# Eight weight slots each for two projections of a fused transformer kernel, loaded behind the projection before them

## What is computed

```python
def hybrid_mixer(h, w_in, ..., w_gdn_proj, sc_conv_w, w_sc_out, w_o):
    p = h @ w_in                                   # q, k, v, z, three short-conv inputs, two gates
    ...
    o = gated_delta_rule_chunked(q, k, v, g, beta) # recurrence, head by head, chunks of 64 tokens
    o = rms_norm(o, gdn_norm_w) * silu(z)
    y_a = o.reshape(b, s, V_W) @ w_gdn_proj        # second projection of the change
    y_b = (gb * causal_depthwise_conv(gc * xin, sc_conv_w)) @ w_sc_out   # first projection
    gate_a = sigmoid(p[..., GA_OFF:GB_OFF]); gate_b = sigmoid(p[..., GB_OFF:IN_COLS])
    return (gate_a * y_a + gate_b * y_b) @ w_o     # third projection

# around it: x = x + g1 * mixer(modulate(rms_norm(x), sh1, sc1)), then an FFN in the same form,
# a final norm, and two further blocks with mixers and FFNs of their own.
# mod = silu(c) @ w_ada + b_ada gives the shifts, scales and gates; w_ada_f those of the first final norm.
```

## Time and profile before

| | us |
|---|---|
| median of three runs | 1551.38 |
| lowest and highest run | 1547.10, 1552.73 |
| device time of the profiled execution | 1547.16 |
| its span | 1545.6 |
| PE busy (share of the span) | 1433.0 (93%) |
| VectorE (DVE) busy | 747.8 (48%) |
| ScalarE (ACT) busy | 644.4 (42%) |
| last instruction of the last head on PE ends | 472.94 |
| second projection on PE starts | 475.50 |
| third projection on PE starts | 527.69 |
| first FFN on PE starts | 563.38 |

### The profile page before, as it was taken

How to read it: one execution, slowest core, us unless ns; L and a number is a source line. 1 busy time by engine, 2 the same in 40 slices (tenths; PEclk the granted TensorE clock), 3 DMA queues, 4 the chain that set the end, 5 groups by cost and what they waited for, 6 DMA issues and landing times.

```text
span 1545.6 us, 27829 instructions
## 1 busy us (share of the span) xinstructions
PE 1433.0 (93%) x10169; PEld 1261.8 (82%) x10169; DVE 747.8 (48%) x1452; ACT 644.4 (42%) x1171; POOL 14.8 (1%) x81
## 2 busy tenths in 40 slices
PE   5999999999998889999979998899998899899997
PEld 2977888887885678899947777799997678799997
DVE  0666656666532144455456543655553122555553
ACT  3454544445322044445364432555542222555542
POOL 3000000000000000000000000000000000000000
PEclk9899999999998989999979999899999889899999
DMA  8666457564553759965639983466564125266562
GB/s 292 178 206 203 150 151 232 187 196 136 166 148 125 214 151 290 273 183 160 173 109 291 282 271 96 137 185 181 162 180 157 29 86 135 70 185 180 167 187 83
DMA packets 400010, 269.89 MB, mean 175 GB/s; under 512 B 9914, under 2 KB 357424, under 8 KB 399936
## 3 DMA queue, kind: packets, MB, share of 16 engines
q1 hardware_dynamic: 399936, 268.83, 58.6%
HBM read 267.75 MB, written 1.05 MB: 174 GB/s over the span
## 4 chain that ended last, share of the span: by engine, by line
PE 76%; DMA 8%; DVE 7%; ACT 4%; issue 2%; SPq 2%; DVEq 0%; ACTq 0%
PE bank L715 16%; PE bank L716 15%; PE bank L717 15%; PE bank L680 5%; DMA w_raw<-in_w_in 4%; PE bank L758 4%; PE bank L651 3%; PE bank L666 2%; PE bank L1080 1%; DMA big<-in_w_ada 1%; DMA ring<-in_w_gdn_proj 1%; PE bank L888 1%; DVE w_low L1658 1%; PE bank L889 1%; PE bank L1112 1%
## 5 line engine op out<-in xcount | busy, mean ns | idle before, releaser
L715 PE MATMUL bank<-h_parts,w_high 128*128 128x256 f32 x1824 | 550.5, 302 | 17.0 <-DVE h_parts L1674 15.4
L716 PE MATMUL bank<-h_parts,w_high 128*128 128x256 f32 x1824 | 523.1, 287 | 0.0
L717 PE MATMUL bank<-h_parts,w_low 128*128 128x256 f32 x1824 | 522.4, 286 | 0.0
L1658 DVE TENSOR_TENSOR w_low<-w_raw,w_high 128x1024 fp32r<-128x1024 f32 (+2 forms) x324 | 359.5, 1122 | 184.2 <-ACT w_high L1223 184.0
L715 PEld LDWEIGHTS bank<-h_parts,w_high 128*128 128x128 f32 x1824 | 355.7, 195 | 43.8 <-issue 25.3
L716 PEld LDWEIGHTS bank<-h_parts,w_high 128*128 128x128 f32 x1824 | 357.5, 196 | 3.9 <-issue 3.6
L717 PEld LDWEIGHTS bank<-h_parts,w_low 128*128 128x128 f32 x1824 | 356.7, 196 | 0.0
L1223 ACT ACTIVATE w_high<-w_raw 128x1024 fp32r<-128x1024 f32 (+2 forms) x324 | 312.6, 973 | 81.4 <-DMA w_raw<-in_w_in 38.0
L1215 ACT ACTIVATE evac<-bank 128x256 f32<-128x256 f32 x140 | 53.9, 385 | 232.9 <-PE bank L717 183.3
L715 PE MATMUL bank<-act_parts,w_high 128*128 128x256 f32 x528 | 149.3, 283 | 0.0
L717 PE MATMUL bank<-act_parts,w_low 128*128 128x256 f32 x528 | 148.6, 281 | 0.0
(11 more groups left out here) (338 smaller groups left out, 1495.6 us busy)
## 6 DMA issues: line engine op xcount, KB each, us to landing
w_raw<-in_ffn_w_in SPq DMA_DIRECT2D x88, 512.0 KB, 3.8
w_raw<-in_w_in SPq DMA_DIRECT2D x72, 512.0 KB, 4.0
ada_w<-in_ada_w SPq DMA_DIRECT2D x34, 1024.0 KB, 5.4
w_raw<-in_w_ffn_in SPq DMA_DIRECT2D x44, 512.0 KB, 6.4
ada_w<-in_w_ada SPq DMA_DIRECT2D x16, 1024.0 KB, 11.5
w_raw<-in_gla_w_in SPq DMA_DIRECT2D x24, 512.0 KB, 6.4
w_raw<-in_ffn_w_out SPq DMA_DIRECT2D x32, 384.0 KB, 3.8
w_raw<-in_ffn_w_out SPq DMA_DIRECT2D x32, 320.0 KB, 3.0
```

Source lines behind the costliest of these rows:

```text
L715: pe.matmul(acc[:, 0:T], hi[:, n, :], x_parts[:, k, 0, :], start=k == 0, stop=False)
L716: pe.matmul(acc[:, 0:T], hi[:, n, :], x_parts[:, k, 1, :], start=False, stop=False)
L717: mm = pe.matmul(acc[:, 0:T], lo[:, n, :], x_parts[:, k, 0, :], start=False, stop=k == kb - 1)
L1658: dve.tensor_tensor(w_low[:, s, 0:m], w_raw[:, s, 0:m], w_high[:, s, 0:m].bitcast(F32), ALU.subtract)\
```

## The change

The second and third projection get eight slots each and are described as one round of eight pieces. The second takes slots 6, 8, 9, 10, which the input projection leaves, and 3, 0, 1, 2, which the first projection leaves block by block; the third takes 12 to 17, and 7 and 11.

```diff
-        st_pa = Stream(KB // 2, 2, 8)
-        st_o1 = Stream(KB // 4, 4, SplitStream.RINGS)
+        st_pa = Stream(1, KB, [6, 8, 9, 10, 3, 0, 1, 2])
+        st_o1 = Stream(1, KB, [12, 13, 14, 15, 16, 17, 7, 11])
```

SP asks for four pieces of the second projection and six of the third straight behind the first projection's, then for the first unit of `ada_w`, then for the other six pieces, and only then for the later units of `ada_w`:

```diff
             load_all(st_pb, wb)
+            load_all(st_pa, wa, range(4))
+            sp.wait_ge(S("ada_rows"), H1)
+            load_all(st_o1, wo, range(6))
...
-            stream(st_pa, lambda i, j: (slot(st_pa.slots[j]), wa[:, :, bass.ds(i * 2 * P + j * P, P)]), extra=ada2)
-            wo = kview(a["w_o"][0])
-
-            stream(st_o1, lambda i, j: (slot(st_o1.slots[j]), wo[:, :, bass.ds(i * 4 * P + j * P, P)]))
+            ada2(0)
+            load_all(st_pa, wa, range(4, KB))
+            load_all(st_o1, wo, range(6, KB))
+            for i in range(1, 4):
+                ada2(i)
```

On PE, seven of the eight matmuls of each of the first two blocks move ahead of the waits for the last head's output and the modulation:

```diff
             pe.wait_ge(S("evacuated"), st_pa.block0 + 3)
+            for j in range(2):
+                block_product(st_pa, 0, j, bank[j], oall, 2, part=range(H1 - 1))
+            pe.wait_ge(S("mod_ready"), 4)
             pe.wait_ge(S("head_out"), H1)
-            pe.wait_ge(S("mod_ready"), 4)
-            stream(st_pa, lambda j: oall, ada=lambda i, j: ada_rows(A_PROJ + i, 0, i, j, first=i == 0))
-            stream(st_o1, lambda j: hT, ready=("mix_ready", 0), norm=1)
+            for j in range(KB):
+                block_product(st_pa, 0, j, bank[j % 2], oall, 2, part=[H1 - 1] if j < 2 else None)
+                ada_rows(A_PROJ + j // 2, 0, j // 2, j % 2, first=j < 2)
+            for j in range(KB):
+                if j == KB - 1:
+                    norm_sum(1, range(KB - 2))
+                block_product(st_o1, 0, j, bank[j % 2], hT, 2, ready=("mix_ready", 0))
+            norm_sum(1, range(KB - 2, KB))
```

More of the change, by code:

```diff
@@ L392, in program @@
         A_HEAD, A_PROJ = 1, 1 + H1
-        A_FFN1 = A_PROJ + st_pa.n
+        A_FFN1 = A_PROJ + 4
         A_GLA = A_FFN1 + 5
@@ L513, in _ @@
             wa, wb = kview(a["w_gdn_proj"][0]), kview(a["w_sc_out"][0])
+            wo = kview(a["w_o"][0])
             load_all(st_pb, wb)
+            load_all(st_pa, wa, range(4))
+            sp.wait_ge(S("ada_rows"), H1)
+            load_all(st_o1, wo, range(6))
             def ada2(i):
                 load_ada(A_PROJ + i, a["w_ada_f"], i * ADA)
-            stream(st_pa, lambda i, j: (slot(st_pa.slots[j]), wa[:, :, bass.ds(i * 2 * P + j * P, P)]), extra=ada2)
-            wo = kview(a["w_o"][0])
-            stream(st_o1, lambda i, j: (slot(st_o1.slots[j]), wo[:, :, bass.ds(i * 4 * P + j * P, P)]))
+            ada2(0)
[3 more added lines that the diff above has]
+                ada2(i)
             def ada3(i, j):
@@ L682, in block_product @@
                         mm.then_inc(S("gemm_done"), 1)
[L684 to L703, removed]
             def split_product(st, i, j, acc, x_parts, ks, kb, ready=None, part=None):
@@ L935, in _ @@
             pe.wait_ge(S("evacuated"), st_pa.block0 + 3)
+            for j in range(2):
+                block_product(st_pa, 0, j, bank[j], oall, 2, part=range(H1 - 1))
+            pe.wait_ge(S("mod_ready"), 4)
             pe.wait_ge(S("head_out"), H1)
-            pe.wait_ge(S("mod_ready"), 4)
-            stream(st_pa, lambda j: oall, ada=lambda i, j: ada_rows(A_PROJ + i, 0, i, j, first=i == 0))
-            stream(st_o1, lambda j: hT, ready=("mix_ready", 0), norm=1)
-            ffn(1, st_f1, st_d1, lambda i, h: ada_rows(A_FFN1 - 1 + i, KB, st_pa.n - 1 + i, h), 2)
+            for j in range(KB):
[6 more added lines that the diff above has]
+            norm_sum(1, range(KB - 2, KB))
+            ffn(1, st_f1, st_d1, lambda i, h: ada_rows(A_FFN1 - 1 + i, KB, 3 + i, h), 2)
             norm_sum(3)
@@ L1384, in out_blocks @@
             def out_blocks(st, sem, base, per, gate):
[L1386 to L1389, removed]
+                for j in range(KB):
+                    act.wait_ge(S(sem), base + j + 1)
+                    c = gate * KB + j
+                    copy_out(st, 0, j, evac[:, j % per, :], 2, scale=mod[:, c:c + 1])
             def out_pairs(st, accs, base, gate):
@@ L1397, in out_pairs @@
                                    scale=mod[:, gate * KB + j:gate * KB + j + 1]).then_inc(S("evacuated"), 1)
[L1400 to L1403, removed]
+            for j in range(KB):
+                act.wait_ge(S("mixed"), j + 1)
+                copy_out(st_pa, 0, j, evac[:, j % 2, :], 2)
             out_blocks(st_o1, "o_added", 0, 4, 2)
@@ L1885, in head1 @@
                         ada_bias(1, 0, H1, len(early))
-                        ada_bias(1, H1, H1 - 1, len(early) + H1 + st_pa.n)
+                        ada_bias(1, H1, H1 - 1, len(early) + H1 + 4)
                     if ch < NCH - 1:
@@ L1912, in _ @@
             dve.wait_ge(S("gated"), 1)
[L1913 to L1921, removed]
+            for j in range(KB):
+                dve.wait_ge(S("evacuated"), st_pa.done(0, j) + 3)
+                dve.tensor_tensor(evac[:, j % 2, :], evac[:, j % 2, :], gates[:, j, :], ALU.mult).then_inc(S("gated"), 1)
+                dve.wait_ge(S("gated"), j + 2)
+                dve.tensor_tensor(hT[:, j, :], hT[:, j, :], evac[:, j % 2, :], ALU.add).then_inc(S("mix_ready"), 1)
+                dve.wait_ge(S("mix_ready"), j + 1)
+                dve.sem_inc(S("mixed"), 1)
             def norm_cols(n):
@@ L1927, in add_blocks @@
             def add_blocks(st, per, sem, first):
[L1929 to L1935, removed]
+                for f in range(KB):
+                    dve.wait_ge(S("evacuated"), st.done(0, f) + 3)
+                    dve.tensor_tensor(xT[:, f, :], xT[:, f, :], evac[:, f % per, :], ALU.add).then_inc(S(sem), 1)
+                    dve.wait_ge(S(sem), first + f + 1)
+                    dve.tensor_tensor(sq[:, f, :], xT[:, f, :], xT[:, f, :], ALU.mult).then_inc(S("norm_sq"), 1)
             def add_down(st, first, batch=None):
@@ L2010, in bias_ffn1 @@
             def bias_ffn1():
-                ada_bias(2, 0, st_pa.n, len(early) + H1)
-                ada_bias(2, st_pa.n, 5, len(early) + H1 + st_pa.n + H1 - 1)
+                ada_bias(2, 0, 4, len(early) + H1)
+                ada_bias(2, 4, 5, len(early) + H1 + 4 + H1 - 1)
             ffn(1, st_f1, st_d1, lambda: ada_copy(2, 2 * A_GLA), bias_ffn1)
@@ L2100, in head2 @@
                 if not gemm:
-                    ada_bias(3, 0, 12, len(early) + H1 + st_pa.n + 12)
+                    ada_bias(3, 0, 12, len(early) + H1 + 4 + 12)
                 dve.wait_ge(S("kv_done"), 3 * c + 2)
```

## The result

Over four runs of each, the changed kernel takes 1529.57 us in the median (1524.54 to 1534.31), the kernel before 1549.24 (1541.69 to 1552.73). The ratio is 0.989, with a 95% interval of 0.9858 to 0.9923. Six further executions on one chip, beside 17 of the kernel before, gave 1527.56 against 1547.20, ratio 0.987 (0.9838 to 0.9901). It is faster by 0.8 to 1.4% by the first interval, 12 to 22 us; 15.6 us were forecast, and the median of 1529.57 lies within the range of 1529 to 1544, at its low end.

What follows compares the result with a forecast made beforehand. PE's path was taken as the bound, with transfer waits and slow-clock starts in the second projection. 37.2 + 0.3 + 1.7 = 39.2 us instead of 54.75 is 15.6 less: 1551.38 - 15.6 = 1535.8 us, range 1529 to 1544.

Steps and rivals of the forecast that it cites:

- What bounds the kernel: Whole kernel: PE carries 76% of the chain, transfers 8%; in the second projection PE pays pauses and slow-clock starts.
- The stretch: From the last head's last matmul to the third projection's first matmul: 54.75 us before, forecast 39.2 us.
- Part 1: Second projection: with new slots and SP order, three waits for pieces and their slow starts go, 12.65 us.
- Part 2: Reload of `ada_w` halves in the second projection: PE waits 0.3 us, bounds 0 and 2.1 us.
- Part 3: Second projection's start: fourteen early matmuls remove a 2.56 us pause; slow clock still loses 1.7 us, bounds 0 and 3.4.
- the 17.55 us: Most that could be gained between the last head's last matmul and the third projection: 54.75 us against 37.2 us undisturbed.
- Part 4: Loops written out, ACT and DVE work at a block's end: zero change; some 1.5 us once if uncovered.
- Rival 1: Second projection: the `ada_w` reload becomes the bound, gain only 7.5 us, 1543.9 us; chance 0.07.
- Rival 2: First projection: its pieces share engines with later transfers, PE stands 18 us, 2.4 us slower, 1553.8 us; chance 0.03.
- Rival 3: SP's queue: a slot comes free late, holding late pieces and `ada_w`; gain 5.7 us, 1545.7 us; chance 0.04.
- the sum: Forecast for the whole change: 37.2 + 0.3 + 1.7 = 39.2 us instead of 54.75, 15.6 us less.

Runs made afterwards that it cites:

- experiment 2: The changed kernel without the fourteen early matmuls ahead of the wait for the last head's output; ratio 0.9912 to the kernel before, median 1534.48 us.
- experiment 4: The kernel before, two slots kept, with both pieces of a round asked for ahead of both halves of `ada_w` on SP; ratio 0.9999.
- experiment 3: The kernel before with only the fourteen matmuls moved ahead of the waits, slots and transfer order as before; ratio 0.9992.
- experiment 5: The changed kernel with eight slots for the second projection only, the third in two rounds in four slots; ratio 0.9877 to the kernel before.
- experiment 1: Both kernels profiled again without any edit: changed kernel ratio 0.987 to the kernel before; kernel before 1546.42 us in one execution.
- experiment 6: The changed kernel with six third-projection pieces asked for one ahead of each later `ada_w` half; ratio 0.9867 to the kernel before.

## Why the prediction was right, point by point

**What bounds the kernel** held: the chain through PE, with the transfers' waits and their slow starts on it. The stretch was forecast at 39.2 us and is 38.5 and 38.65.

**Part 1, slots and order.** 12.65 us forecast, 12.68 measured by experiment 2. That the two agree to hundredths is luck: against the second profile of the kernel before (53.1 us) it is 11.0. That SP's order and not bandwidth made the waits was half of it: in experiment 4 the other order on two slots gains nothing, and in experiment 3 a piece asked for 3.5 us sooner takes 3.4 us longer to land. The transfers ended at about 465 where the prediction had 471. They had begun 3.3 us sooner, at 420.17 and not at 423.5, the two `ada_w` halves among them came at 380 GB/s, which is an estimated 1.7 us, and the rest is rounding in the forecast. The pieces of the first projection were not pushed back; the landing of its pieces stays ahead of their blocks, and PE has no wait for `w_sc_out` on the chain. That the third projection's slots pay nothing (experiment 5) the prediction didn't say, but it gave them no price either.

**Part 2, the reload of `ada_w`.** 0.3 us forecast. The first late half was issued at 478.82, landed 5.2 us later (the value taken), and PE reached it at 484.04: the wait is within 0.1 us. The 0.2 us less come from the issue, 0.06 us after the use and not 0.2, and from the two records between the half rows, 0.63 us and not 0.43. From the second on there is no wait to speak of, as forecast, and the slack is larger than the prediction had it: the second half landed 3.0 us after the first, not 3.6, and at 380 GB/s it takes an estimated 2.8 us of transfer. This was the mis-sized term, and it errs to the safe side. The Trainium skill's line of 2.0 us plus bytes at 436 GB/s ("DMA: Bandwidth & Descriptors", "Anatomy of one DMA — SWDGE (gpsimd) path") gives an estimated 4.4 us for a half, by a fit on GpSimd's path; here 5.0 to 5.2 us were measured with nothing ahead of it, so the measurement stands.

**Part 3, the early matmuls.** 1.7 us lost to the clock were forecast between bounds of 0 and 3.4. In the two profiles of the changed kernel the 30 records at the start take 7.96 and 8.14 us, 1.5 and 1.7 us more than the 6.47 us (all three by the chain) in the kernel of experiment 5, which is equal there and shows no fall. The place of the fall was not as forecast: the prediction had it 0.5 us behind the end of the last head's last matmul, and it came 0.5 us before that end in the first profile and 3.5 us before it, at 467.8, in the second, which made the last head longer too (86.3 us from the first projection to the third instead of 85.2). So the value of 1.7 us is partly luck; the bounds held. That this part shortens nothing without part 1 (experiment 3) the prediction did not say: it split the 17.55 us by start times and added the parts, which is right for both together only.

**Part 4** held for the stretch: no wait on ACT or DVE entered the chain. Behind the third projection it was not zero but a gain of 0.3 us, by the shorter way from the last block to the norm sum (experiment 1).

**The rivals.** Rival 1 did not come: experiment 6, which adds five pieces, 2.6 MB, to the same 28 us, still costs only 1.0 us. Rival 2 is excluded by the chain. Rival 3 is excluded by SP's queue: the last piece is issued by 461, and no block waits.

**The size.** The median fell by 19.7 us in both comparisons, 4.1 more than the sum. The interval of the second one reaches down to 15.3 us, so the sum isn't contradicted. The stretch and the 0.3 us behind it give 16.5; the rest has no place that is shown to be the change's, and parts with an equal program differ by as much (experiment 1). That the median of 1529.57 still lies in the range is narrow, by 0.6 us: it is 6.2 us under the 1535.8 forecast, 4.1 of them from the gain and 2.1 because the kernel before, with a fourth execution, has a median of 1549.24 and not 1551.38.

## What to carry to other kernels

Two kinds of refill, each into a buffer just freed and both in one queue, were late in either of the two orders tried here: whichever came second was waited for. What helped was to give one of the two its own slots and to ask for it where the queue is idle (here the last 30 us of the phase before), so that it leaves the queue to the other. An order that asks for each load the moment its buffer is free was not tried.

Work that can be moved ahead of a wait is worth keeping for exactly that wait. In the stretch fourteen early matmuls brought 3.5 us once nothing else was late and nothing while transfers set the pace. Spent in gaps before the wait they could have covered, they brought no more than behind the last head (85.8 us from first to third projection, against 85.2 and 86.3, and 88.6 without them).

## What the runs showed of the hardware

- TensorE's clock fell behind some pauses and not behind others of the same length: of three pauses of 2.60 to 2.61 us in one profile (the kernel before, second profile), two were followed by 1.7 us of loss each and one by none. It also fell inside the last head, where PE had no pause of over 0.5 us (at 469.3 and 467.8 in the two profiles of the changed kernel). Two profiles of one kernel differed by 1.7 us in the same stretch, in the kernel before (54.75 and 53.1 us) and in the one with eight matmuls in the gaps (84.2 and 82.5). Over a longer part two profiles with the same program there differed by 4.2 us, at a granted clock of 0.95 and 0.98.
- Transfers with rows of 512 bytes ran at 290 GB/s and those with rows of 2 KB at 380 GB/s, on the same queue, with the DMA engines busy throughout (428 to 440 and 449 to 454 us of the changed kernel). The cause of the difference was not isolated.
- A half of `ada_w` (1024 KB) landed 5.0 to 5.2 us after its issue with an empty queue, and after a median of 8.0 us in experiment 6, with a piece asked for just ahead of all but the first.
